# Who adds up the squares of the split norms: VectorE instead of GpSimd, in a one-core chain of two transformer blocks

## The reference

```python
def rms_norm_2(x, g):
    xf = x.astype(jnp.float32)
    y = xf * lax.rsqrt(jnp.mean(xf * xf, axis=-1, keepdims=True) + EPS)
    return (y * g.astype(jnp.float32)).astype(x.dtype)
...
        x = x + ml[2] * yl
        x = x + ml[5] * sq_relu_mlp(modulate(rms_norm_2(x, norm2_g[i]), ml[3], ml[4]), mlp_w1[i], mlp_w2[i])
...
    return rms_norm_2(x, final_g)
```

## Time and profile before

| What | Value |
|---|---|
| median of 3 runs | 4377.08 us (4374.86 to 4383.14) |
| the profiled execution, its time | 4373.73 us |
| its span in the trace | 4371.9 us |
| instructions in the trace | 42557 |
| chain that ended last, share of PE | 71% |
| chain, share of DVE / ACT / POOL | 3% / 1% / 1% |

### The profile page before, as it was taken

One profiled execution on the slowest core, in us unless ns is written; L12 is line 12 of the kernel. 1 busy time (PEld: TensorE's weight loads), 2 busy tenths in 40 slices (PEclk: granted clock), 3 DMA queues, 4 the chain that ended last, 5 costly groups with the idle time before them and its releaser, 6 DMA issues.

```text
span 4371.9 us, 42557 instructions
## 1 busy us (share of the span) xinstructions
PE 4141.8 (95%) x16792; PEld 2745.5 (63%) x16792; DVE 1822.2 (42%) x3139; ACT 973.2 (22%) x2176; POOL 427.3 (10%) x305
## 2 busy tenths in 40 slices
PE   9999978799998899999999888999999999999998
PEld 4357544244554455665655457888845888858887
DVE  2653256443276122212010394665264666414433
ACT  1141116232155121100010253201123202112020
POOL 0000000110000000000000001111140212202112
PEclk8999969689999899999999999999999999999999
DMA  3203320202100222223111211355210344312221
GB/s 121 72 24 111 110 64 12 77 16 75 36 9 10 66 77 96 103 89 116 58 59 57 69 43 39 136 172 173 78 58 0 135 169 158 101 39 94 80 95 41
DMA packets 209203, 343.16 MB, mean 78 GB/s; under 512 B 19888, under 2 KB 79696, under 8 KB 208976
## 3 DMA queue, kind: packets, MB, share of 16 engines
q1 hardware_dynamic: 190048, 322.11, 21.3%
q10 hardware_dynamic: 17424, 10.48, 0.9%
q0 software_dynamic: 1536, 7.87, 0.7%
HBM read 334.41 MB, written 6.03 MB: 78 GB/s over the span
## 4 chain that ended last, share of the span: by engine, by line
PE 71%; DVE 3%; issue 1%; ACT 1%; POOL 1%; ACTq 0%; DMA 0%; DVEq 0%; POOLq 0%
PE psum L1419 26%; PE psum L1267 26%; PE psum L1372 5%; PE psum L1376 3%; PE psum L1530 2%; PE psum L1484 2%; PE psum L1605 2%; PE psum L1509 1%; DVE small L2383 1%; POOL arena L2604 1%; PE psum L1229 1%; ACT arena L1870 1%; DVE psum L2378 1%; PE psum L1592 1%; DVE arena L2398 0%
## 5 line engine op out<-in xcount | busy, mean ns | idle before, releaser
L1267 PE MATMUL psum<-H,ring 128*128 128x512 f32 (+1 forms) x3312 | 1152.7, 508 | 32.4 <-issue 17.0
L1267 PEld LDWEIGHTS psum<-H,ring 128*128 128x128 f32 x3312 | 630.0, 192 | 537.9 <-issue 489.7
L1419 PE MATMUL psum<-arena,ring 128*128 128x256 f32 x1536 | 342.8, 380 | 2.8 <-ACT arena L1717 2.8
L2153 DVE SCALAR_TENSOR_TENSOR arena<-ring,cond,arena 128x512 f32<-128x512 f32 x448 | 319.5, 752 | 8.0
L1419 PEld LDWEIGHTS psum<-arena,ring 128*128 128x128 f32 x1536 | 290.4, 190 | 44.0 <-ACT arena L1717 5.2
L1419 PE MATMUL psum<-arena 128*128 128x256 f32 x1152 | 256.3, 379 | 0.4
L2136 DVE TENSOR_TENSOR mods<-psum,vec 128x4 f32<-128x4 f32 (+1 forms) x48 | 7.8, 162 | 586.8 <-PE psum L1229 585.9
L2383 DVE TENSOR_REDUCE small<-psum 128x1 f32<-128x768 f32 (+7 forms) x352 | 204.0, 614 | 114.0 <-PE psum L1491 50.2
L1858 ACT ACTIVATE arena<-psum,small 128x768 f32<-128x768 f32 (+7 forms) x336 | 204.5, 613 | 162.5 <-DVE small L2383 127.3
L1484 PE MATMUL psum<-arena 64*128 64x512 f32 (+4 forms) x960 | 218.3, 496 | 22.9 <-ACT arena L1858 18.4
L1419 PEld LDWEIGHTS psum<-arena 128*128 128x128 f32 x1152 | 218.6, 190 | 30.3 <-ACT arena L1722 0.7
(11 more groups left out here) (226 smaller groups left out, 4811.5 us busy)
## 6 DMA issues: line engine op xcount, KB each, us to landing
ring<-in_mlp_w SPq DMA_DIRECT2D x64, 2048.0 KB, 8.5
ring<-in_ada_w SPq DMA_DIRECT2D x48, 2048.0 KB, 7.9
ring<-in_na_qkv SPq DMA_DIRECT2D x6, 2048.0 KB, 7.9
ring<-in_pw SPq DMA_DIRECT2D x6, 2048.0 KB, 8.0
ring<-in_ab_in SPq DMA_DIRECT2D x5, 2048.0 KB, 7.9
ring<-in_cd_in SPq DMA_DIRECT2D x4, 2048.0 KB, 10.2
ring<-in_at_qkv SPq DMA_DIRECT2D x3, 2048.0 KB, 7.7
ring<-in_ab_out SPq DMA_DIRECT2D x2, 2048.0 KB, 8.2
```

The lines of the kernel that those rows point to most:

```text
L1267: last = nc.tensor.matmul(out, lhs, rhs, start=(k == 0), stop=(k == len(t.pairs) - 1))
L1419: last = nc.tensor.matmul(bank(at, HALF, HALF * m), w[:, i, P * m:P * m + P], x[:, i, :], start=(opens and m == 0 and i == 0), stop=(i == ...
L2153: ins = nc.vector.scalar_tensor_tensor(partial[:, v, :], w[:, k, :], cond[:, k, v:v + 1], partial[:, v, :], ALU.mult, ALU.add)
```

## The change

`sum_squares` moves from POOL's program to DVE's, with the same 98 adds on the same tiles. It is entered into DVE's table `side` under `nsq`, where `nothing` stood; so in the projections DVE makes the add of tile k directly behind writing X's tile k, ahead of whatever else stands behind that tile. In the last unit of an MLP two calls of `steps_after` are new, for the squares that stand behind products 2 and 4. POOL keeps L2571 and L2593.

```diff
@@ -2098,8 +2098,10 @@
                         sum_u2()
                         c11()
                         sum_u3()
+                        steps_after(2)
                         c21_sum()
                         c21()
+                        steps_after(4)
                         steps_after(5)
                         c12()
                         c22()
@@ -2325,6 +2327,21 @@
+            def sum_squares(normed, at):
+
+                half, k = at
+                if k == 0:
+                    return
+                dve.wait_ge(squares_ready, normed.sq0[half] + k + 1)
+                if k > 1:
+                    settle()
+                total = normed.sq[:, 0, halves[half]]
+                ins = nc.vector.tensor_tensor(total, total, normed.sq[:, k, halves[half]], ALU.add)
+                if k < KD - 1:
+                    step(ins)
+                else:
+                    ins.then_inc(sumsq_ready, 1)
@@ -2359,7 +2376,7 @@
-                        nsq=nothing, nsum=normed_inverse, nspread=normed_scale, wsums=next_sums, gains=gains_of)
+                        nsq=sum_squares, nsum=normed_inverse, nspread=normed_scale, wsums=next_sums, gains=gains_of)
@@ -2532,22 +2549,6 @@
-            def sum_squares(normed, half, k):
-
-                nonlocal pool_count
-                if k == 0:
-                    return
-                pool.wait_ge(squares_ready, normed.sq0[half] + k + 1)
-                if k > 1:
-                    pool.wait_ge(pool_steps, pool_count)
-                total = normed.sq[:, 0, halves[half]]
-                ins = nc.gpsimd.tensor_tensor(total, total, normed.sq[:, k, halves[half]], ALU.add)
...
@@ -2571,16 +2572,11 @@
                         if i + 1 < len(us):
                             third_sum(us[i + 1])
                         n_units = u["id"]
-                        if u["last"]:
-                            for kind, normed, at in listed[1] + listed[2] + listed[4]:
-                                sum_squares(normed, *at)
                         pool.wait_ge(u3_out, n_units + 1)
...
@@ -2592,9 +2588,6 @@
-                        if u["last"]:
-                            for kind, normed, at in listed[5] + listed[3]:
-                                sum_squares(normed, *at)
...
@@ -2607,8 +2600,6 @@
                     for kind, job, i in rotations:
-                        if kind == "nsq":
-                            sum_squares(job, *i)
                         if kind != "swap":
```

More of the change, by code:

```diff
@@ L2573, in _ @@
                     us, tmp = st["units"], st["tmp"]
-                    last = us[-1]
-                    listed = {p: [x for x in last["after"][p] if x[0] == "nsq"] for p in last["order"] if p in last["after"]}
                     third_sum(us[0])
```

## The result

The changed kernel took 4388.48 us in the median of 17 runs, against 4380.11 us of the kernel before in 17 runs beside it. The ratio is 1.002, with a 95% interval of 1.0012 to 1.0027: 5 to 12 us slower; the medians are 8.4 us apart. The forecast was 4380.6 us in a range up to 4386, so the time lies 2.5 us above the range. Of the 7.9 us between it and the measured median, 3.0 are the base: three runs had the kernel before at 4377.08, seventeen have it at 4380.11. The other 4.9 are a loss of 8.4 us that was forecast as 3.5.

What follows compares the result with a forecast made beforehand. PE, busy 95% of the span, was taken as the bound. Waits of 0.50 + 0.24 + 2.79 = +3.5 us on the runs' median of 4377.08 gave 4380.6 us, range 4374.5 to 4386, verdict no change.

Steps and rivals of the forecast that it cites:

- six places: End of `na_o`, ends of `pw2` and `ft_w`, and three MLP ends: the only places where PE was forecast to lose time.
- The price of an add: On DVE, each add of squares was taken as 0.42 us, from L2188 of the same shape; bounds 0.33 and 0.72 us.
- End of `na_o`, +0.50: Weight sums behind tile 14 start 0.91 us later, L2002 gives 0.41 us back; tile 15 and PE's MLP start 0.50 later.
- Ends of `pw2` and `ft_w`, +0.12 each: Tile 15 is 0.50 or 0.4 us later, the last add gives 0.33 back; rounded up to 0.12 us each, together 0.24.
- Last units of the MLPs, +0.93 each: Five adds hide under DVE's wait for PE; two more delay scaling half 0 by 0.93 us, three times, 2.79 us.
- The sum, +3.5 by the waits: Whole kernel: 0.50 + 0.24 + 2.79 = 3.5 us slower; some 3.0 or 9.7 us at the add-price bounds.
- the step from the waits to the time: Whole kernel: later PE idle times hang on engines waiting for PE, so the 3.5 us of waits is the whole loss.
- rival 3: Clock falls after MLP-end idle, 1.7 us a stretch; 4384 or more, or a slow add: 0.12, half beyond 8.8 us.
- The base: The forecast added its 3.5 us to 4377.08 us, the median of runs of the kernel before.
- Rivals 1 and 2: 1: projection ends gain 1.4 us, net +1.4, 4378.5 (0.13). 2: projection adds reach PE, up to 51 us, 4428 (0.03).

Runs made afterwards that it cites:

- proj_only: Against the kernel before: DVE adds the squares in the four projections only, POOL keeps its adds in the MLPs' last units; ratio 1.0007, tail 1655.1 us.
- mlp_only: Against the kernel before: DVE adds the squares in the MLPs' last units only, POOL keeps those of the projections; ratio 1.0008, tail 1660.0 us.
- before_delay: The kernel before, all adds on POOL, plus one useless DVE instruction ahead of scaling half 0 at each MLP end; ratio 1.0015, tail 1664.3 us.
- late_adds: The changed kernel with half 0 scaled before the adds of tiles 6 and 7 at the MLP ends; ratio to the kernel before 1.0004, tail 1654.6 us.
- late_mlp: Against the kernel before: MLP adds on DVE, half 0 scaled before those of tiles 6 and 7; projections' adds stay on POOL; ratio 1.0005.

## Why the prediction was wrong

The sign, the places and most of the terms were right. It named six places where PE would feel the change and found nothing in the other adds; the equal stretches ahead of tile 14, proj_only and mlp_only bear that out.

- **The price of an add**, 0.42 us from L2188: measured 0.425.
- **End of `na_o`, +0.50**: measured 0.50, with the 0.41 us that L2002 gives back. The Trainium skill, SBUF — State Buffer, section "Who interferes with whom", would have had 0.55 back; the row was nearer.
- **Ends of `pw2` and `ft_w`, +0.12 each**: measured 0.23 and 0.22. The terms given were 0.50 later and 0.33 back, which is 0.17, or 0.07 with the lower value for tile 15.
- **Last units of the MLPs, +0.93 each**: measured 0.57. The term left out that DVE's last two writes of X (L2047) had been held up 0.47 us by POOL's adds, which are gone; before_delay and late_adds show 1.35 us with and 0.88 us without them. It is the effect that I had seen at L2002, and rows 7 showed it: 1.35 us for two instructions whose median is 0.48 each. The two remaining adds cost 0.96; the last 0.08 are overlaps.
- **The sum, +3.5 by the waits**: measured 2.7.
- **What failed is the step from the waits to the time: "Later idle times of PE hang on engines that wait for PE, so it stays."** It put the clock at nothing in the sum and left it to rival 3, at 0.12. The longer idle time at the two inner MLP ends brings TensorE's clock down for longer, and once more behind `ft_w`: by the windows 7.0, 7.0 and 8.6 us lost in the three profiles after, 1.8 in each before. That is 5.7 us more on average, twice all waits together. With the waits' 2.7 it makes 8.4 of the 8.8 us between the tails. Rival 3 had the price of one stretch right, 1.7 us, and asked for four more of them to pass the 0.2%; against a mean of 16 us at half clock in the tails before there are 11 to 18 us more, so three to five came. Against it stood only that the second MLP end has the same wait and that the stretch is one of six changed places, and the whole was read from one window of one profile. In that profile the second end is at 1.00; in the second and third profile of the same kernel the stretch is at the second end and not at the first.
- **The base.** The forecast added to a median of three runs that seventeen runs put 3.0 us higher.
- **Rivals 1 and 2** did not come: tile 15 is late and costs PE at all three projections; DVE's take of a tile is still released by PE (2.06 us of idle time ahead of tile 14).

Open is why, without fillers, the clock falls at the third window only with both halves of the change or a still longer idle time, why late_mlp has a stretch at both MLP ends with 2.0 us of idle time, and what decides where it falls once the MLP ends are filled.

## What to carry to other kernels

In a kernel bound by TensorE, an added stall of half a microsecond is not priced by its length: look at the granted clock around the stall in several profiles. Where it already falls below 1.00 in some of them, a longer stall can cost a multiple of itself, as 2.7 us of waits cost 8.8 here. Where an engine that is waited for gets more work, put that work behind the step that releases TensorE; this one turn of order gave back what the change had cost, to within the noise (1.0004, 0.9996 to 1.0013). And compare two kernels from an instruction that both run in the same way: the three tails of a kernel lay 1.4 and 3.2 us apart, where a ratio from twelve runs left 4 us open to either side.

## What the runs showed of the hardware

- Around two restarts of PE the granted clock was at 1.2 instead of 2.4 GHz for 10.2 to 13.7 us together in four profiles with 3.1 to 3.6 us of idle time ahead of each, and for 3.4 us in five profiles with 2.0 to 2.5 us. One profile of either kind had 6.8 us (mlp_only and late_mlp). The longer waits themselves were 1.1 us at the two places in the changed kernel.
- Useless matmuls in the idle time kept it at 1.00 there (six windows of six, in three kernels), and in each of the three it fell for 3.4 us at a later place.
- SCALAR_TENSOR_TENSOR with two inputs in SBUF (L2047) is held up by GpSimd's adds as TENSOR_TENSOR is: 1.35 instead of 0.88 us for two; a TENSOR_TENSOR of 128 by 512 (before_delay) took 1.21 us beside them.
- The same code ahead of `na_o` took from 2716.7 to 2732.1 us in 14 profiles, for the most part through the clock: in the first two it was at half clock for 328 and 331 us there, in mlp_only, the slowest, for 355.
